# The first norm of a hybrid trunk kernel: statistics on the token rows, x loaded first, h in one pass

## What is computed

```python
def rmsnorm(x, g):
    y = x * lax.rsqrt(jnp.mean(x * x, axis=-1, keepdims=True) + EPS)
    return y * g

mod = jax.nn.silu(cvec) @ prm["w_mod"][l] + prm["b_mod"][l]      # (1024) @ (1024, 6144)
shift1, scale1, gate1, shift2, scale2, gate2 = jnp.split(mod, N_MOD, axis=-1)
h = rmsnorm(x, prm["norm_pre"][l, 0]) * (1.0 + scale1) + shift1
mix = even_mixer(h, prm["ev_w_in"][j], ...)                      # h @ w_in comes first
```

## Time and profile before

| | us |
|---|---|
| median of 3 runs | 1945.16 (1945.13 to 1947.17) |
| the profiled execution | 1939.72 |
| its span | 1937.9 |
| TensorE busy | 1846.0 (95%) |
| VectorE busy | 961.6 (50%) |
| ScalarE busy | 844.2 (44%) |
| mean granted clock of TensorE | 0.996 of full speed |

### The profile page before, as it was taken

The page is one execution under the profiler, slowest core; times in us unless marked ns, Lnnn a source line. Parts: engine busy times, 40 slices in busy tenths (PEclk is TensorE's granted clock), DMA queues, the critical chain, the costliest instruction groups (busy, mean ns, idle before and its releaser), DMA issues.

```text
span 1937.9 us, 36137 instructions
## 1 busy us (share of the span) xinstructions
PE 1846.0 (95%) x14744; PEld 1702.8 (88%) x14744; DVE 961.6 (50%) x1558; ACT 844.2 (44%) x1464; POOL 87.7 (5%) x126
## 2 busy tenths in 40 slices
PE   6999988998999999999999999999999999999998
PEld 3999866666789999999999897776899999999997
DVE  4433355556646555235555753434365553255555
ACT  4545333335756444123445743443464441144453
POOL 0000234430000000000000000000000000000000
PEclk9999999999999999999999999999999999999999
DMA  7221455551021222222224311111211222122243
GB/s 283 66 67 55 156 201 199 196 180 55 2 70 44 66 76 79 74 65 76 75 83 140 106 37 36 27 32 33 66 41 58 76 75 87 55 76 74 79 135 114
DMA packets 238720, 170.21 MB, mean 88 GB/s; under 512 B 20138, under 2 KB 230284, under 8 KB 232332
## 3 DMA queue, kind: packets, MB, share of 16 engines
q1 hardware_dynamic: 238604, 168.54, 28.0%
HBM read 165.08 MB, written 3.44 MB: 87 GB/s over the span
## 4 chain that ended last, share of the span: by engine, by line
PE 84%; DVE 6%; ACT 5%; issue 3%; POOL 1%; DMA 0%; SPq 0%; ACTq 0%; DVEq 0%
PE ps L1999 45%; PE ps L2075 15%; PE ps L2032 4%; PE ps L2193 2%; PE ps L2628 2%; PE ps L2665 2%; PE ps L2203 2%; PE ps L2624 2%; PE ps L2350 1%; PE ps L2498 1%; PE ps L2383 1%; PE ps L2475 1%; ACT w_hi L789 1%; POOL level_b L737 1%; DVE scores L1793 1%
## 5 line engine op out<-in xcount | busy, mean ns | idle before, releaser
L789 ACT ACTIVATE w_hi<-w_raw 128x1024 fp32r<-128x1024 f32 (+4 forms) x187 | 198.7, 1062 | 560.7 <-PE ps L1999 435.8
L1364 DVE TENSOR_TENSOR w_lo<-w_raw,w_hi 128x1024 fp32r<-128x1024 f32 (+4 forms) x191 | 234.2, 1227 | 377.1 <-ACT w_hi L789 376.7
L1999 PE MATMUL ps<-h_hi,w_hi 128*128 128x322 f32 x1648 | 381.4, 313 | 3.2 <-ACT conv L979 1.7
L1999 PE MATMUL ps<-h_lo,w_hi 128*128 128x322 f32 x1648 | 380.1, 312 | 0.0
L1999 PE MATMUL ps<-h_hi,w_lo 128*128 128x322 f32 x1648 | 378.0, 310 | 0.0
L1999 PEld LDWEIGHTS ps<-h_hi,w_hi 128*128 128x128 f32 x1648 | 278.1, 189 | 4.8 <-ACT conv L1190 2.0
L1999 PEld LDWEIGHTS ps<-h_hi,w_lo 128*128 128x128 f32 x1648 | 279.1, 189 | 0.0
L1999 PEld LDWEIGHTS ps<-h_lo,w_hi 128*128 128x128 f32 x1648 | 279.0, 189 | 0.0
L2075 PE MATMUL ps<-g_hi,w_hi 128*128 128x322 f32 x352 | 110.7, 314 | 3.0 <-DVE g_lo L1842 2.0
L2075 PE MATMUL ps<-g_lo,w_hi 128*128 128x322 f32 x352 | 109.6, 311 | 0.0
L2075 PE MATMUL ps<-g_hi,w_lo 128*128 128x322 f32 x352 | 109.1, 310 | 0.0
(11 more groups left out here) (373 smaller groups left out, 3398.8 us busy)
## 6 DMA issues: line engine op xcount, KB each, us to landing
w_raw<-in_ffn_w_up SPq DMA_DIRECT2D x88, 512.0 KB, 3.7
w_mod_raw<-in_w_mod SPq DMA_DIRECT2D x40, 1024.0 KB, 5.7
w_raw<-in_ffn_w_down SPq DMA_DIRECT2D x48, 704.0 KB, 4.3
w_raw<-in_ev_w_in SPq DMA_DIRECT2D x18, 512.0 KB, 3.6
w_mod_first<-in_w_mod SPq DMA_DIRECT2D x8, 1024.0 KB, 15.6
w_raw<-in_ev_w_out SPq DMA_DIRECT2D x8, 512.0 KB, 3.5
w_raw<-in_od_w_out SPq DMA_DIRECT2D x8, 512.0 KB, 3.6
w_raw<-in_od_w_kv_up SPq DMA_DIRECT2D x24, 128.0 KB, 2.3
```

The costliest lines, as they stand in the source:

```text
L789: act.activation(WH[slot][:, 0:k, :], RAW[slot][:, 0:k, :], ACT.Copy).then_inc(w_hi, 1)
L1364: dve.tensor_tensor(WL[slot][:, 0:k, :], RAW[slot][:, 0:k, :], WH[slot][:, 0:k, :].bitcast(F32), ALU.subtract).then_inc(w_lo, 1)
L1999: last = pe.matmul(out, w_of(k, wi), x_of(k, xi, i), start=(k == 0 and p == 0), stop=(k == ks - 1 and p == 2))
```

## The change

- The twelve vector loads move from SP's queue to ScalarE's, in front of everything else that ScalarE does. SP now issues constants, x, six w_mod pieces, weight blocks 0 and 1, and the last two w_mod pieces.
- The norm statistics are taken on the token rows as loaded, tokens on the partitions: ScalarE squares three tiles with an accumulated sum, VectorE two with one instruction each. The root is then taken of 128x5 values.
- ScalarE scales two tiles into `x_unit_rows`, VectorE three. TensorE turns the five scaled tiles into `x_unit` and then the five unscaled ones into `x_t`: 80 transposes where there were 40. It uses two pairs of banks by turns (6, 7 and 2, 3). The w_mod products come after all of them.
- The squares by chunk, their sums, `norm_stat`, the root over 644 columns and `x_unit` (line 1529) are gone.
- ScalarE writes `h_hi` straight from `x_unit` with gain and shift, two pieces for each chunk. VectorE applies gain and shift once more for itself, into `x_affine`, and subtracts `h_hi`. GpSimd zeroes the gaps of `h_hi` and `h_lo`.
- VectorE's two `w_rest` come ahead of its copy of the modulation row. `keep_busy` now stands behind w_mod's pieces 4 to 7 (3, 3, 3, 2 calls of the product) and five times before h, on bank 1.

The diff, cut to this part (the rest renumbers semaphore counts):

```diff
-    NORMS = (("first", KD, 1), ("l2", 8, 8), ("on", 4, 8), ("cq", C_Q // P, 1), ("ckv", C_KV // P, 1))
+    BY_ACT, BY_DVE = (0, 1, 2), (3, 4)
+    NORMS = (("first", 0, 0), ("l2", 8, 8), ("on", 4, 8), ("cq", C_Q // P, 1), ("ckv", C_KV // P, 1))
...
+    XS = [place(f"x_unit_rows{t}", [D], R_W + D * t) for t in range(NT)]
+    XSQ = [place(f"x_row_sq{s}", [D], R_T + 2 * al(TW) * s) for s in range(2)]
+    XNA = [place(f"x_affine{s}", [TW], R_A + al(TW) * s) for s in range(2)]
+    XSUM = place("x_row_sum", [8], R_SC)
+    XRST = place("x_row_rstd", [8], R_SC + 8)
...
-            def rows(dst, r0, src):
-                sp.dma_start(dst[r0:r0 + src.shape[0], :], src).then_inc(S("vec_landed"), 16)
...
-            rows(VR[0], V_C, a["c_ctx"].rearrange("(k p) -> k p", p=P))
...
             for t in range(NT):
                 src = a["x_prompt"][0] if t == 0 else a["x_sample"][0, (t - 1) * P:t * P, :]
                 sp.dma_start(XR[t][:, :], src).then_inc(S("x_landed"), 16)
 
             wm = [a["w_mod"][l].rearrange("(k p) m -> p k m", p=P) for l in range(2)]
             for k in range(KD):
+                if k == KD - 2:
+                    for n in range(2):
+                        load(n, ein_v[:, :, (6 + n) * P:(7 + n) * P])
                 sp.dma_start(MWS[k][:, :], wm[0][:, k, 0:2 * D]).then_inc(S(f"mod_landed{k}"), 16)
 
-            for n in range(23):
+            for n in range(2, 23):
                 if n < E_AB:
...
-            pool.wait_ge(S("rows_turned"), 2 * NT)
             pool.wait_ge(S("mod_done"), KD)
+            zero_gaps(S("gpsimd_filled"), *H2)
+            pool.wait_ge(S("rows_turned"), RT0)
...
+            def rows(dst, r0, src):
+                act.dma_start(dst[r0:r0 + src.shape[0], :], src).then_inc(S("vec_landed"), 16)
+
+            rows(VR[0], V_C, a["c_ctx"].rearrange("(k p) -> k p", p=P))
...
+            rows(VR[3], 8, a["b_mod"].rearrange("l (m p) -> (l m) p", p=P))
             act.preload_act_table_set("natural_log_exp_and_others")
 
             act.wait_ge(S("vec_cols"), 2)
             act.activation(SCE[:, :], VC[:, 0:16], ACT.Exp, scale=-1.0).then_inc(S("exp_c"), 1)
 
-            for t in range(NT):
-                act.wait_ge(S("rows_turned"), 2 * t + 1)
-                act.activation(X[:, 0:4, TILES[t]:TILES[t] + P], bank(6).rearrange("p (k c) -> p k c", c=P),
+            act.wait_ge(S("x_landed"), 16 * NT)
+            for x, t in enumerate(BY_ACT):
+                if x:
+                    act.wait_ge(S("norm_sq"), x)
+                act.activation(XSQ[0][:, :], XR[t][:, :], ACT.Square, accum_out=XSUM[:, t:t + 1]).then_inc(S("norm_sq"), 1)
+            act.wait_ge(*filled("eps"))
+            act.wait_ge(S("norm_sq"), len(BY_ACT))
+            act.wait_ge(S("norm_sum"), len(BY_DVE))
+            act.activation(XRST[:, 0:NT], XSUM[:, 0:NT], ACT.Ln, scale=1.0 / D, bias=EPSC[:, 0:1]).then_inc(S("norm_ln"), 1)
+            act.wait_ge(S("norm_ln"), 1)
+            act.activation(XRST[:, 0:NT], XRST[:, 0:NT], ACT.Exp, scale=-0.5).then_inc(S("norm_rstd"), 1)
+            act.wait_ge(S("norm_rstd"), 1)
+            for t in BY_DVE:
+                act.activation(XS[t][:, :], XR[t][:, :], ACT.Copy, scale=XRST[:, t:t + 1]).then_inc(S("h_shifted"), 1)
+            for y in range(2 * NT):
+                dst, t = ((XN, X)[y // NT], y % NT)
+                act.wait_ge(S("rows_turned"), 2 * y + 1)
+                act.activation(dst[:, 0:4, TILES[t]:TILES[t] + P], bank((6, 2)[y % 2]).rearrange("p (k c) -> p k c", c=P),
                                ACT.Copy).then_inc(S("rows_copied_a"), 1)
-            act.wait_ge(S("rows_copied_a"), NT)
-            act.wait_ge(S("rows_copied_v"), NT)
-            act.wait_ge(*filled("eps"))
-            squares("first", lambda k: X[:, k, :], lambda k: None, KD)
-            rstd("first", D)
             hi(0)
             hi(1)
             act.wait_ge(S("mod_ready"), 1)
+            act.wait_ge(*filled("h_gaps"))
+            act.wait_ge(S("rows_copied_a"), NT)
+            act.wait_ge(S("rows_copied_v"), NT)
             for k in range(KD):
-                act.wait_ge(S("h_scaled"), k // 2 + 1)
                 for c, c0, c1 in CONDS:
-                    last = act.activation(XN[:, k, c0:c1], XN[:, k, c0:c1], ACT.Identity, bias=MOD[0][:, 2 * k + c:2 * k + c + 1],
+                    last = act.activation(Hh[:, k, c0:c1], XN[:, k, c0:c1], ACT.Identity, bias=MOD[0][:, 2 * k + c:2 * k + c + 1],
                                           scale=PA[0][0][:, 2 * k + c:2 * k + c + 1])
-                last.then_inc(S("h_shifted"), 1)
-                act.wait_ge(S("h_shifted"), k + 1)
-                act.activation(Hh[:, k, :], XN[:, k, :], ACT.Copy).then_inc(S("h_hi"), 1)
+                last.then_inc(S("h_hi"), 1)
...
+            for x in XNA:
+                dve.memset(x[:, 0:1], 0.0)
+                dve.memset(x[:, P0 + PROMPT:S0], 0.0)
+                dve.memset(x[:, S0 + SAMPLE:TW], 0.0)
...
-            for t in range(NT):
-                dve.wait_ge(S("rows_turned"), 2 * t + 2)
-                dve.tensor_copy(X[:, 4:8, TILES[t]:TILES[t] + P], q4(bank(7))).then_inc(S("rows_copied_v"), 1)
-            dve.wait_ge(*filled("eps"))
-            sums("first", KD)
-            dve.wait_ge(*of("rstd", "first", 1))
-
-            def x_unit(j):
-
-                dve.tensor_tensor(XN[:, 2 * j:2 * j + 2, :], X[:, 2 * j:2 * j + 2, :],
-                                  RST[:, :].unsqueeze(1).broadcast_to([P, 2, TW]), ALU.mult).then_inc(S("h_scaled"), 1)
-            x_unit(0)
-            x_unit(1)
+            dve.wait_ge(S("x_landed"), 16 * NT)
+            for x, t in enumerate(BY_DVE):
+                if x:
+                    dve.wait_ge(S("norm_sum"), x)
+                dve.tensor_tensor_reduce(XSQ[1][:, :], XR[t][:, :], XR[t][:, :], 1.0, 0.0, ALU.mult, ALU.add, XSUM[:, t:t + 1]
+                                         ).then_inc(S("norm_sum"), 1)
+            dve.wait_ge(S("norm_rstd"), 1)
+            for t in BY_ACT:
+                dve.tensor_scalar(XS[t][:, :], XR[t][:, :], XRST[:, t:t + 1], None, ALU.mult).then_inc(S("h_scaled"), 1)
+            for y in range(2 * NT):
+                dst, t = ((XN, X)[y // NT], y % NT)
+                dve.wait_ge(S("rows_turned"), 2 * y + 2)
+                dve.tensor_copy(dst[:, 4:8, TILES[t]:TILES[t] + P], q4(bank((7, 3)[y % 2]))).then_inc(S("rows_copied_v"), 1)
+            w_rest(0)
+            w_rest(1)
             dve.wait_ge(S("mod_done"), KD)
             dve.tensor_copy(MROW0[:, :], bank(0)).then_inc(S("mod_rows"), 1)
-            x_unit(2)
             dve.wait_ge(S("mod_turned"), 1)
             mod_columns(0, 0, 5, "mod_cols")
             gains(0, 0, 1, "mod_ready")
-            w_rest(0)
-            x_unit(3)
-            w_rest(1)
+            dve.wait_ge(S("rows_copied_a"), NT)
+            dve.wait_ge(S("rows_copied_v"), NT)
             for k in range(KD):
+                if k >= 2:
+                    dve.wait_ge(S("h_lo"), k - 1)
+                for c, c0, c1 in CONDS:
+                    q = 2 * k + c
+                    step(dve.tensor_scalar(XNA[k % 2][:, c0:c1], XN[:, k, c0:c1], PA[0][0][:, q:q + 1], MOD[0][:, q:q + 1],
+                                           ALU.mult, ALU.add)) if c else dve.tensor_scalar(
+                        XNA[k % 2][:, c0:c1], XN[:, k, c0:c1], PA[0][0][:, q:q + 1], MOD[0][:, q:q + 1], ALU.mult, ALU.add)
                 dve.wait_ge(S("h_hi"), k + 1)
-                dve.tensor_tensor(Hl[:, k, :], XN[:, k, :], Hh[:, k, :].bitcast(F32), ALU.subtract).then_inc(S("h_lo"), 1)
+                dve.tensor_tensor(Hl[:, k, :], XNA[k % 2][:, :], Hh[:, k, :].bitcast(F32), ALU.subtract).then_inc(S("h_lo"), 1)
...
-            pe.wait_ge(S("x_landed"), 16 * NT)
-            for t in range(NT):
+            for y in range(2 * NT):
+                t = y % NT
+                if y == 0:
+                    pe.wait_ge(S("h_scaled"), len(BY_ACT))
+                    pe.wait_ge(S("h_shifted"), len(BY_DVE))
                 for part, sem in ((0, "rows_copied_a"), (1, "rows_copied_v")):
-                    if t:
-                        pe.wait_ge(S(sem), t)
+                    if y >= 2:
+                        pe.wait_ge(S(sem), y - 1)
+                    b = ((6, 7), (2, 3))[y % 2][part]
                     for k in range(4):
-                        last = turn(PS[:, (6 + part) * 512 + P * k:(6 + part) * 512 + P * k + P],
-                                    XR[t][:, (4 * part + k) * P:(4 * part + k + 1) * P])
+                        last = turn(PS[:, b * 512 + P * k:b * 512 + P * k + P],
+                                    (XS, XR)[y // NT][t][:, (4 * part + k) * P:(4 * part + k + 1) * P])
                     last.then_inc(S("rows_turned"), 1)
             pe.wait_ge(S("silu_c"), 1)
             for k in range(KD):
-                if k == KD - 2:
-                    norm_stat("first")
```

(7 more changed lines are left out.)

50 lines of the change are left out of this document (25 added, 25 removed).

## The result

| | before | after |
|---|---|---|
| median, run side by side (16 runs each) | 1944.15 us | 1949.05 us |
| ratio after / before | | 1.0024, 95% interval 1.0013 to 1.0035 |
| profiled execution | 1939.72 | 1950.56 |
| its span | 1937.9 | 1948.8 |
| mean granted clock of it | 0.996 | 0.995 |

The change makes the kernel slower, by 4.9 us in the medians. I had forecast no change. The time lies inside the range, but the direction is one to which I gave 0.15. The wait that did it is the third rival's: the vectors starve.

What follows compares the result with a forecast made beforehand. TensorE was taken as the bound from the turns on. The steps put the first product at 44.1 us against 44.26, about -0.2, giving a 1945.0 us median; range from just under 1941.5 to 1949.3.

Steps and rivals of the forecast that it cites:

- third rival: Vector loads starve behind x and w_mod; slower from a landing at 12.8 us on, 1949.3 and up; chance 0.08.
- Vectors: Vector loads on ScalarE's queue, sharing engines with x: landing taken at 8.7 us, 10 with some latency.
- Loads: x_prompt issued at 1.19 us instead of 5.70; x landing between 9.9 and 11.2, taken as 10.8.
- Statistics, scaling: Square-sums and root done at 15.35 us, five tiles scaled by 17.7; VectorE 0.75 a tile, high bound 1.23.
- Turns: TensorE's 80 transposes take 11.0 us, to 28.7, with 21 of them at half speed.
- Rival 2: All TensorE turns stay slow: 15.7 us instead of 11.0, 4.7 later, 1949.7; chance 0.07.
- w_mod: Stream ends at 34.5 us; TensorE reaches the last piece at 38.85, without waiting for its data.
- rival 1: DMA stream of w_mod stays the bound: first product at 39.75 us, 4.5 earlier, 1940.6; chance 0.10.
- From there to h, and the pace: Last piece to first product of h at 44.1 us; then TensorE-bound, 14.5 for the pair, one ScalarE pass saved worth nothing.
- The range: Whole time from just under 1941.5 us to 1949.3, the high end from VectorE's high bounds and vectors at 10.

Runs made afterwards that it cites:

- e2: Changed kernel with the vectors' turn, the exponential and silu moved behind the five scaled tiles; median 1944.24 us, ratio to before 0.9994.
- e7: Changed kernel with h made in two passes again, as before; first product of h at 51.92 us, no whole time given.
- e9: Kernel before with 18 more products of constants ahead of the first pair; median 1950.18 us, ratio to before 1.0026.
- e6: Kernel before with only the twelve vector loads moved to ScalarE's queue; one execution, 1950.35 us.
- e1: Changed kernel with the vector loads back on SP's queue ahead of x; median 1945.37 us, ratio to before 0.9992.
- e3: Changed kernel without the 11 products of constants between w_mod's pieces; one execution, 1952.52 us.
- e12: Kernel before with 8 more products of constants ahead of the first pair; median 1953.71 us, ratio to before 1.0058.
- e10: e5 with 8 more products of constants ahead of the first pair; median 1942.24 us, ratio to before 0.9990.
- e4: Changed kernel with SP holding w_mod back until the vectors have landed; one execution, 1944.50 us.
- e5: Changed kernel reordered: x then vectors on SP's queue, silu off the path, unscaled turns replacing constant products between pieces; median 1948.31 us, ratio to before 1.0009.
- e11: e5 run again, on another chip; median 1948.07 us, ratio to before 1.0016.

## Why the prediction was wrong

The mechanism, TensorE bound from the first turn on with each step after the other, was right. One step failed, *Vectors*: I took their landing at 8.7, with 10 as the worst shared case, and it was 16.4. The clock of the prediction against that of the changed kernel:

| step | forecast | measured |
|---|---|---|
| vectors landed | 8.7 | 16.4 |
| from there to all tiles scaled | 9.0 (to 17.7) | 8.55 (to 25.02) |
| 80 turns | 11.0 | 10.56 |
| seven pieces, nine constant products | 10.15 | 10.9 |
| from the last piece to the first product | 5.25 | 5.29 |
| first product | 44.1 | 51.77 |
| first pair | 14.5 | 14.5 |

44.1 + 7.77 (the turn at 16.47) - 0.45 - 0.44 + 0.75 + 0.04 is 51.77. Everything but the first line was within 0.8 us.

- *Loads.* x_prompt was issued at 1.19 as said. x landed near 12.0 and not 10.8 (e2, where the squares wait for x alone), 0.8 outside the bound of 11.2. It cost nothing here, since the vectors were later.
- *Vectors.* Two arguments carried the 8.7. One was that many vector rows are issued before x flows, from a start at about 2.6. That counted loads and not rows: 360 of the 482 rows are in the last four loads, issued from 3.97 to 6.45, and they moved from 8.0 us on. The other was a wait of one 4 KB row of x for each vector row. From 8 us on the two queues did go nearly packet for packet. But from 10 us on the rows beside were more and more w_mod's of 8 KB (71 from 10 to 12 us, 100 from 12 to 14), which the sum left out. An estimate with both put right, from my own terms: 360 rows are 22.5 for each engine, and behind 8 KB rows at 420/16 GB/s, 0.31 us each, they take 7.0 us, so from 8.0 they are in by 15.0. By 14 us all but nine packets were through; these took until 16.3. I wrote that no row showed two queues sharing, and then bounded the unknown within 2.8 us. The Trainium skill, DMA: Bandwidth & Descriptors, Queues, rings and completion order, has an engine drain a whole packet of several descriptors before it goes on to the next queue. The one for one from 8 to 14 us, with work on both queues, is not what I had made of that rule. The one in seven before 4 us and one in 2.5 from 4 to 8 (153 to 384) can't decide it, because the loads that moved then hold at most 36 rows each and the others were still being issued. Why 360 rows issued from 3.97 on first moved at 8.0, where before the same loads were in by 7.20, stays open.
- *Statistics, scaling.* Right. VectorE's multiplication took 0.69 us a tile (2.08 for three) where I had 0.75, and the high bound of 1.23 is out. The exponential and silu were done 2.05 and 3.15 after the vectors' turn began, as read from the earlier trace rows.
- *Turns.* Right. The first 40 took 6.02 and the second 4.40, so the slow lengths ended within the first 40. Rival 2 is out. The Trainium skill, TensorE: Matmul & The Clock Gate, PE-mode transpose, states that transposes do not count for the clock. For this kernel the trace disagrees: nothing but transposes ran there when the weight loads went from 0.19 us each (six in 1.14 us from 25.02 on) to 0.11.
- *w_mod.* Right in kind: no wait for it, which leaves out rival 1. The DMA share falls from 1.00 (30 to 33 us) to 0.02 (34 to 35), so the stream ended near the 34.5 that I took. A piece with three constant products took 2.49 and not 2.17.
- *From there to h, and the pace.* Right. That one pass over h is worth nothing was not quite so: e7 shows 0.8 ahead of F and 0.4 behind it.
- *The range.* Rival 3 had its decision point (12.8) and, at the first product, its price (each us costs one) right, and I gave it 0.08. Its argument against, that most are issued by 4 us, holds for eight of the twelve loads and 122 of the 482 rows. By its price 16.4 is 7.7 later, or 1952.7, outside the range. The medians say 4.9, as they do for e9, and the clock moves the medians of these programs by that much in either direction. So it is luck that the time lies inside the range. I had left the granted clock out of the sum, with 1.00 in every window I read at the start, and had not looked at the stage from 210 us on.

What is shown: the queue alone starves the vectors (e6), and the starved vectors cost 5.0 us of F (e2) or 4.4 with x's gain given up (e1). The rest of the 7.5, 2.5 us, is the new way itself. The nine constant products between the pieces cost 4.9 (e3), so everything else of the new way together gains some 2.4. That the later F makes the longer time is supported and not shown: a delay of about that size gives the same loss in the median (e9, 4.9) and at equal clock (6.1 to 6.4), but e12's smaller delay lost more. What stays open: why the number of dips differs so much between programs with the same work in that stage, and so what e12 measured. No version is shown to beat the kernel before; e10 is the nearest, with an interval that reaches past 1.

## What to carry to other kernels

A load moved to a second queue "beside" a deep stream need not land beside it: 0.25 MB took until 16.4 us here, and until 7.2 ahead on the same queue. Ask what is in flight on the engines when it arrives. Count its rows and not its loads, from the moment at which the last large load is issued, and let each wait behind the largest row of the stream. If it must be early, put it ahead on the same queue (e1), or else make sure that nothing on the way stands behind it in any engine's order (e2 did that with the same loads). Filler work placed in a wait becomes cost when the wait goes. And when a stage later in the program runs partly at the lower clock, a gain of a few us at the start is no longer readable from one median: compare the moment itself in the trace, and run a kernel that is only delayed, as a control.

## What was not expected of the hardware

- 0.25 MB on ScalarE's queue took until 16.4 us beside SP's stream (604 packets, at most 12.1% of the engines' time in the windows above), and until 12.7 beside x alone (e4). The same rows queued behind x on SP's queue were in at 12.5 to 13.9 (e10, e5, e11). Beside SP's rows they moved about one for one, whether those had 4 KB or 8.
- SP's issue of two weight loads took 15.26 us behind six w_mod pieces, and the last two w_mod pieces could only be issued at 22.9. It did no harm, since TensorE came to them later still. It would bind a kernel that reached them before.
- The mean granted clock of a program over twelve runs lay between 0.9918 (e11) and 0.996 (e1) with the same work after the start, by short dips to 1.2 GHz, most of them in the stage of small products. By the line above that is worth an estimated 6 us of the median here, more than the change itself, and adding useless products made one kernel 5.8 us faster (e10 against e11) and another 9.0 slower (e12).
